# First block of a fused two-block forward pass: split projections, modulation weights on 32-column tiles, attentions begun after three slots

## The chip, the cores and the metric

The kernel runs on one core of one Trainium2 chip. The metric is device time in microseconds (us). The core has a matrix engine (TensorE, PE in the views; its weight loads are listed as PEld), VectorE (DVE), ScalarE (ACT), GpSimd (POOL) and SyncE (SP), which issues the loads. All five run their own instruction streams and meet at semaphores.

## The reference, cut to what matters

Two blocks of two layers each follow one another on an activation of 256 tokens by 1024 features. The change touches the first block alone:

```python
def first_block(x, c, ada_w, ada_b, norm_g, ab_w_in, ab_w_out, ..., c_w_in, c_w_out, c_sink, final_g):
    cs = jax.nn.silu(c)
    for layer in range(DEPTH):                                  # 2 layers
        mod = cs @ ada_w[layer] + ada_b[layer]                  # 1024 -> 3072, one row
        shift, scale, gate = jnp.split(mod, 3, axis=-1)
        h = rms_norm(x, norm_g[layer]) * (1.0 + scale[:, None, :]) + shift[:, None, :]
        if layer % 2 == 0:  y = even_mixer(h, ab_w_in, ab_w_out, ...)
        else:               y = odd_mixer(h, c_w_in, c_w_out, c_sink)
        x = x + gate[:, None, :] * y
    return rms_norm(x, final_g)
```

`even_mixer` projects h to 4096 features, runs 8 heads of a banded attention with three patterns (A) and 4 heads of a differential attention (B, two score maps each), multiplies by `silu(g)` and projects back. `odd_mixer` projects to 2560 features, runs 16 banded heads with a sink, gates and projects back. Everything is float32.

## The kernel before, in words

**Slots.** Every weight is cut into slots of 1 MB (128 partitions by 2048 values), in the order of `NAMES`, and SyncE loads them one after another into a ring of four (`RING`); slot n+4 is issued when TensorE has signalled slot n (`slot_done`). Of the first block: `ada0_*` and `ada1_*` (12 each, the modulation vector of a layer), `even0..15` and `even_out0..3`, `odd0..9` and `odd_out0..3`. Those of the second block begin with L0. Besides these, SyncE issues x (1 MB) ahead of slot 5, and constants of 0.88 MB ahead of slot 7 and 0.56 MB ahead of slot 8.

**A slot on TensorE.** In the first block a projection slot is 16 float32 matmuls of 128x128 by 256 (`pe_features`, or `pe_tokens` where tokens go to partitions). The trace has each float32 matmul as two records. An `ada` slot is 8 such matmuls with a broadcast vector as the stationary side; VectorE takes the diagonal of each 128x128 half (`dve_mod_slot`).

**Split slots.** The second block writes each float32 as a rounded high part plus a low part and multiplies high by high, high by low and low by high, 48 matmuls of one record each (`pe_split`). For it ScalarE casts the slot to `w_split` (two buffers, `act_highs`; the cast for split slot w waits until split slot w-2 is done), and VectorE subtracts and leaves the low part in the ring (`dve_lows`). `act_slot` and `dve_slot` take a slot's result and then cast and subtract ahead; `dve_slot` subtracts first (up to the next slot), and takes the result then. h itself comes as `h_split` (high) and `hT_rounded` (low).

**Attention as a pipeline.** `pe_attention` walks over pairs of score maps. Step k has on TensorE the scores of pair k (`sc`), the values of pair k-2 (`yv`), the transposes of pair k-1 (`tp`), and then filler slots from the table `FILL`. VectorE has in step k the bias and row minimum of pair k (`att_area`, L461), the results of the filler of step k-1, the scaling of pair k's probabilities (L476 to L486) and the product of the finished chunk (L1920). ScalarE has the filler's results, the exponentials (L428) and the copies of the transposes (L442). GpSimd builds the bias tables (L508 to L511), two heads ahead. There are 8 pairs in each of the two attentions, so steps 0 to 9.

**Order around the change.** ada0_0 to ada0_8; norm; even0 to even12; the even attention with even13 to 15 and nine ada slots as filler; sums for the norm of the differential heads; ada1_6 and 7; `even_out`; norm; odd0 to odd5; the odd attention with odd6 to 9 and ada1_9 to 11; `odd_out`; then the second block with L0sbq.

## Time and profile before

| what | us |
|---|---|
| device time, median of 3 runs (1488.1 to 1491.31) | 1490.55 |
| the profiled execution | 1490.07 |
| its span in the trace | 1488.2 |
| first even projection begins | 44.8 |
| even attention begins, after 13 slots | 134.8 |
| even_out begins, after ada1_6 and ada1_7 | 220.8 |
| odd projections begin | 256.9 |
| odd attention, from its first scores | 299.5 |
| odd_out begins | 373.0 |
| second block begins (L0sbq) | 417.9 |

The page gives busy times and shares of the span. The chain of waits in order of time gives the piece of work that held the end at each moment: a piece on TensorE means that TensorE itself was the limit there, one on another engine that TensorE waited for it. What comes after 417.9 us is the second block, which keeps its code and its slots.

### The profile page before, as it was taken

To read this page: it belongs to the slowest core of one execution; us is meant where nothing else is said; L and a number is where in the kernel's file an instruction comes from. 1 tells how busy PE (TensorE), PEld (TensorE's weight loads), DVE (VectorE), ACT (ScalarE), POOL (GpSimd) and SP (SyncE) were. 2 spreads that over 40 slices of the span, in tenths; PEclk is the share of its full clock that TensorE was granted. 3 is DMA by queue.
4 is the path that set the end of the run, shared out by engine and by line. 5 is a ranking of instruction groups with operands and counts; after the bars stand their busy time and mean duration, and the time that the engine had idled before them with its cause. 6 is when DMAs were issued, how large, how long until landed. Compare 5 with 4: busy or idle time off the path is not lost.

```text
span 1488.2 us, 21174 instructions
## 1 busy us (share of the span) xinstructions
PE 1419.3 (95%) x8756; PEld 1243.8 (84%) x8756; DVE 795.6 (53%) x1156; ACT 623.2 (42%) x821; POOL 195.2 (13%) x130
## 2 busy tenths in 40 slices
PE   8999999998989999999999999899998999999997
PEld 7888788875879898898888888798998888888885
DVE  1102663067164777944775554436778637755543
ACT  1202322044237566621464443476567223644432
POOL 1002310043000034123020000000240231200000
PEclk9999999998989999999999999999999999999999
DMA  9544354433223443301445555333333203454551
GB/s 363 203 166 142 142 207 157 145 114 114 99 103 139 142 147 137 142 29 57 147 179 184 177 191 190 121 142 142 142 142 114 85 29 116 170 195 171 192 178 55
DMA packets 30048, 216.23 MB, mean 145 GB/s; under 512 B 3328, under 2 KB 3584, under 8 KB 4096
## 3 DMA queue, kind: packets, MB, share of 16 engines
q1 hardware_dynamic: 29952, 214.87, 40.1%
q8 instruction: 69, 1.13, 0.3%
q14 instruction: 27, 0.22, 0.0%
HBM read 213.81 MB, written 1.05 MB: 144 GB/s over the span
## 4 chain that ended last, share of the span: by engine, by line
PE 88%; DVE 5%; ACT 4%; issue 2%; DMA 0%; POOL 0%; DVEq 0%; SPq 0%; ACTq 0%
PE pj L520 59%; PE yv L520 13%; PE sc L520 9%; PE tp L520 4%; PE tp L411 1%; ACT w_split L627 1%; DVE rw L1281 1%; PE tp L1458 1%; DVE ring_rounded L636 1%; DVE att_area L461 1%; ACT att_area L428 0%; DVE rstd L683 0%; DMA ring<-weights 0%; DVE hT L685 0%; ACT probsT L442 0%
## 5 line engine op out<-in xcount | busy, mean ns | idle before, releaser
L1617 DVE TENSOR_TENSOR ring_rounded<-ring,big_rounded 128x2048 fp32r<-128x2048 f32 x62 | 142.1, 2292 | 96.0 <-ACT big_rounded L1548 95.8
L636 DVE TENSOR_TENSOR ring_rounded<-ring,w_split 128x2048 fp32r<-128x2048 f32 x68 | 163.1, 2404 | 41.6 <-ACT w_split L627 40.0
L520 PE MATMUL pj<-h_split,w_split 128*128 128x256 f32 x992 | 143.9, 298 | 15.2 <-ACT h_split L1553 10.1
L520 PEld LDWEIGHTS pj<-h_split,w_split 128*128 128x128 f32 x992 | 128.8, 197 | 25.9 <-issue 19.7
L520 PE MATMUL pj<-hT,ring 128*128 128x256 f32 x672 | 147.3, 380 | 1.7 <-DVE mod_raw L1375 1.2
L1548 ACT CAST big_rounded<-ring 128x2048 fp32r<-128x2048 f32 x66 | 125.8, 1906 | 51.3 <-PE pj L520 49.8
L520 PEld LDWEIGHTS pj<-hT,ring 128*128 128x128 f32 x672 | 126.9, 190 | 19.9 <-issue 3.0
L627 ACT CAST w_split<-ring 128x2048 fp32r<-128x2048 f32 x68 | 129.2, 1903 | 21.0 <-PE pj L520 12.9
L520 PE MATMUL pj<-h_split,ring_rounded 128*128 128x256 f32 x992 | 127.8, 282 | 0.0
L520 PE MATMUL pj<-yT,ring 128*128 128x256 f32 x512 | 118.7, 386 | 4.7 <-DVE yT L1329 2.5
L520 PEld LDWEIGHTS pj<-h_split,ring_rounded 128*128 128x128 f32 x992 | 122.6, 191 | 0.0
L520 PEld LDWEIGHTS pj<-yT,ring 128*128 128x128 f32 x512 | 96.8, 193 | 19.8 <-DVE yT L1329 2.9
L520 PE MATMUL pj<-hT_rounded,w_split 128*128 128x256 f32 x864 | 112.5, 283 | 0.0
L520 PEld LDWEIGHTS pj<-hT_rounded,w_split 128*128 128x128 f32 x864 | 107.8, 192 | 0.0
L1023 POOL TENSOR_TENSOR big<-big 128x512 f32<-128x512 f32 x16 | 31.1, 1946 | 494.1 <-DVE big L962 480.8
L520 PE MATMUL pj<-ring,cs 128*128 128x256 f32 x384 | 88.2, 388 | 7.7 <-DMA ring<-weights 6.4
L520 PEld LDWEIGHTS pj<-ring,cs 128*128 128x128 f32 x384 | 74.2, 195 | 18.5 <-issue 8.3
L1350 DVE COPY big<-pj 128x512 f32<-128x512 f32 x11 | 7.6, 689 | 117.5 <-PE pj L520 117.4
L520 PE MATMUL pj<-big_rounded 128*128 128x512 f32 x176 | 69.1, 393 | 0.0
L520 PE MATMUL sc<-big_rounded 128*128 128x512 f32 x176 | 69.0, 392 | 0.0
L1346 ACT ACTIVATE big<-pj 128x512 f32<-128x512 f32 x23 | 13.7, 597 | 123.6 <-PE pj L520 123.6
L510 POOL TENSOR_SCALAR first_block<-first_block 128x384 f32<-128x384 f32 x24 | 28.0, 1168 | 268.0 <-DVE stat L467 124.1
(312 smaller groups left out, 2374.8 us busy)
## 6 DMA issues: line engine op xcount, KB each, us to landing
ring<-weights SPq DMA_DIRECT2D x200, 1024.0 KB, 4.8
xT<-x_t SPq DMA_DIRECT2D x1, 1024.0 KB, 7.0
out_t<-hT SPq DMA_DIRECT2D x1, 1024.0 KB, 3.9
con<-constants SPq DMA_DIRECT2D x1, 896.0 KB, 9.5
aux<-small SPq DMA_DIRECT2D x1, 832.0 KB, 6.4
first_block<-constants SPq DMA_DIRECT2D x1, 576.0 KB, 9.9
level_masks_sb<-levels SPq DMA_DIRECT2D x1, 448.0 KB, 6.0
con<-constants SPq DMA_DIRECT2D x1, 128.0 KB, 5.1
```

The source lines that it names most:

```text
L411: last = nc.tensor.transpose(tp[m["t"] % 2][:, jt * SEQ + it * P:jt * SEQ + (it + 1) * P], probs[:, m["g"] % 4, it, jt * P:(jt + 1) * P], ...
L461: ins = nc.vector.tensor_tensor_reduce(probs[:, m["g"] % 4, it], sc[m["g"] % 2][:, it * SEQ:(it + 1) * SEQ], table[:, P - it * P:P - it * ...
L510: pool.do(nc.gpsimd.tensor_scalar(bias0[:, :], C("dist"), m["slope"], None, ALU.mult))
L520: return nc.tensor.matmul(out, lhsT, rhs, start=start, stop=stop, skip_group_check=True)
L627: act.post(nc.scalar.copy(w_split[:, w % 2], ring[:, idx % RING]), s["w_high"])
L636: dve.post(nc.vector.tensor_tensor(ring_r[:, at], ring[:, at], w_split[:, w % 2].bitcast(F32), ALU.subtract), s["w_low"])
L1023: pool.tell(nc.gpsimd.tensor_tensor(d, b, b[:, :, n - 1:n].to_broadcast([P, 512 // (2 * n), 2 * n]), ALU.subtract), s["hgrn_diff"])
L1281: dve.tell(nc.vector.tensor_tensor(rw[:, kind, T * NH:(T + 1) * NH], quarters((sc + tp)[(2 * kind + T) % 4]), C("before" if kind < 2 else ...
L1346: free(act, nc.scalar.activation(dst, b[:, :], ACT.Copy, scale=scale), name)
L1458: last = nc.tensor.transpose(tp[j % 2][:, (2 * c + T) * P:(2 * c + T + 1) * P], by_token(j, T)[:, c * P:(c + 1) * P], C("ident"))
L1548: act.tell(nc.scalar.copy(w_high(i), ring[:, w_at(t, i) % RING]), s["ffn_high"])
L1617: e.tell(engine.tensor_tensor(w_low(t, i), w, value(w_high(i)), ALU.subtract), signal)
```

## The change

It has five parts.

1. All projection slots of the first block (16 even, 4 even_out, 10 odd, 4 odd_out) become split slots, with casts on ScalarE and subtractions on VectorE. h is shifted by ScalarE straight into `h_split`, and VectorE makes its low part. The attention's output chunks are split into `y_high` (in `big2`) and `y_low` (in `yT_rounded`) as they are finished.
2. The ada slots come as pairs that share one bank of 512 columns' sums: each half has 4 of the 8 row blocks, and each of its 16 matmuls has 32 output columns and 128 moving columns, on column tile j of 4. VectorE takes four diagonals of 32 per pair.
3. The even attention begins after even0, 2, 4 (and even1 as filler of step -1), the odd one after odd4, 5, 0. The others are filler in the steps, with waits (`NEEDED`) on what a pair needs. ada0_8 goes from ahead of the projections into step 3.
4. The subtractions for the next filler group are made ahead in the first block too (`AHEAD`).
5. The final product of the differential heads is made per chunk.

```diff
 FILL = {
-    "even": {-1: ["even12"], 0: ["even13"], 1: ["ada0_9"], 2: ["even14"], 3: ["ada0_10"], 4: ["ada0_11", "ada1_0"],
-             5: ["even15"], 6: ["ada1_1", "ada1_2"], 7: ["ada1_3"], 8: ["ada1_4"], 9: ["ada1_5"],
-             EVEN_TAIL: ["ada1_6"], EVEN_TAIL + 1: ["ada1_7"]},
-    "odd_norm": {0: ["ada1_8"]},
-    "odd": {0: ["odd6"], 1: ["odd7"], 2: ["odd8"], 3: ["odd9"], 4: ["ada1_9"], 5: ["ada1_10"], 6: ["ada1_11"]},
+    "even": {-1: ["even1"], 0: ["even3", "even12"], 1: ["even6", "even8"], 2: ["even5", "even13"],
+             3: ["even10", "ada0_8", "ada0_9"], 4: ["even7", "even9"], 5: ["ada0_10", "ada0_11", "even14"],
+             6: ["even11"], 7: ["ada1_0", "ada1_1"], 8: ["ada1_2", "ada1_3"], 9: ["ada1_4", "ada1_5"],
+             EVEN_TAIL: ["even15"], EVEN_TAIL + 1: ["ada1_6", "ada1_7"]},
+    "odd_norm": {0: ["ada1_8", "ada1_9"]},
+    "odd": {0: ["odd1"], 1: ["odd6"], 2: ["odd2"], 3: ["odd7"], 4: ["odd3"], 5: ["odd8"], 6: ["odd9"],
+            8: ["ada1_10"], 9: ["ada1_11"]},
...
-CHAIN = ("stick", "moba", "hgrn", "rwkv")
-GROUPS = [(phase, k, FILL[phase][k]) for phase in CHAIN for k in sorted(FILL[phase])]
-AHEAD = {phase: {} for phase in CHAIN}
-for (phase_, k_, _), (_, _, next_) in zip(GROUPS, GROUPS[1:]):
-    if "branch" not in next_[0]:
+GROUPS = [(phase, k, at[k]) for phase, at in FILL.items() for k in sorted(at)]
+AHEAD = {phase: {} for phase in FILL}
+for (phase_, k_, _), (next_phase, _, next_) in zip(GROUPS, GROUPS[1:]):
+    if "branch" not in next_[0] and (phase_ == next_phase or phase_ in ("stick", "moba", "hgrn")):
         AHEAD[phase_][k_] = next_[-1]
+EVEN_FIRST, ODD_FIRST = ("even0", "even2", "even4"), ("odd4", "odd5", "odd0")
+NEEDED = {"even": {0: ("even0", "even2"), 2: ("even1", "even3", "even4"), 4: ("even5", "even6", "even8"),
+                   6: ("even7", "even9", "even10"), 8: ("even11",)},
+          "odd": {0: ("odd4", "odd0"), 2: ("odd1", "odd5"), 4: ("odd2",), 6: ("odd3",)}}
...
-    add("ada0_", 9)
-    add("even", 12)
+    add("ada0_", 8)
+    names.extend(EVEN_FIRST)
     names.extend(FILL_ORDER["even"])
     add("even_out", 4)
     names.extend(FILL_ORDER["odd_norm"])
-    add("odd", 6)
+    names.extend(ODD_FIRST)
...
-    return name[0] == "L" and not any(part in name for part in ("branch", "ffn", "down"))
+    return not any(part in name for part in ("ada", "branch", "ffn", "down"))
...
+    if "ada" in n:
+        return ada_part(n) % 2
...
+    put("quad", i[:, None] % 32 == np.arange(32)[None, :])
...
+                for name in NEEDED.get(phase, {}).get(k, ()):
+                    evacuated(pe, name)
...
+        def act_y_high(act, chunk):
+            act.post(nc.scalar.copy(y_high[:, chunk], yT[:, chunk]), s["y_high"])
+
+        def dve_y_low(dve, chunk):
+            dve.take(s["y_high"])
+            dve.post(nc.vector.tensor_tensor(yT_r[:, chunk], yT[:, chunk], value(y_high[:, chunk]), ALU.subtract),
+                     s["y_low"])
...
+                if phase in NEEDED and 3 <= k < 3 + len(placed(phase)):
+                    m = placed(phase)[k - 3]
+                    act.eng.wait_ge(y_out, m["u"] + 1)
+                    act_y_high(act, m["chunk"])
...
+                if phase in NEEDED and 4 <= k < 4 + len(placed(phase)):
+                    dve_y_low(dve, placed(phase)[k - 4]["chunk"])
...
+        def act_h_shift(act):
 
             for k in range(KC):
-                act.take(s["h_scaled"])
-                act.post(nc.scalar.activation(hT[:, k], hT[:, k], ACT.Identity, bias=mod[:, k:k + 1]), s["h_ready"])
+                act.take(s["h_to_split"])
+                act.post(nc.scalar.activation(hh[:, k], hT[:, k], ACT.Identity, bias=mod[:, k:k + 1]), s["h_high"])
+
+        def dve_norm_shift(dve, name):
+
+            dve.take(s["norm_root"])
+            dve.do(nc.vector.reciprocal(rstd[:, 1], rstd[:, 0]))
+            for k in range(KC):
+                dve.post(nc.vector.scalar_tensor_tensor(hT[:, k], xT[:, k], mod[:, 8 + k:9 + k], rstd[:, 1], ALU.mult,
+                                                        ALU.mult), s["h_to_split"])
+            dve_lows(dve, IDX[name])
+            for k in range(KC):
+                dve.take(s["h_high"])
+                dve.post(nc.vector.scalar_tensor_tensor(hT_r[:, k], hT[:, k], mod[:, k:k + 1], value(hh[:, k]), ALU.add,
+                                                        ALU.subtract), s["h_low"])
...
-            for m in range(2):
-                ins = nc.vector.tensor_tensor_reduce(diag[:, :], b[:, m * P:(m + 1) * P], C("ident"), 1.0, 0.0, ALU.mult,
-                                                     ALU.add, mod_raw[:, 2 * i + m:2 * i + m + 1])
-                if m == 0:
+            i = ada_part(name)
+            for m in range(4):
+                ins = nc.vector.tensor_tensor_reduce(diag[:, 0:32], b[:, m * 32:(m + 1) * 32], C("quad"), 1.0, 0.0,
+                                                     ALU.mult, ALU.add, mod_raw[:, 2 * i - 2 + m:2 * i - 1 + m])
+                if m < 3:
...
-                idx = IDX[name]
-                pe_open(pe, name)
-                for k in range(KC):
-                    last = matmul(bank_of(name)[:, 0:SEQ], cs[:, k:k + 1].to_broadcast([P, P]), slot(idx)[:, k],
-                                  k == 0, k == KC - 1)
+                idx, half = IDX[name], ada_part(name) % 2
+                w = ring[:, idx % RING].rearrange("p (k j n) -> p k j n", k=4, j=4)
+                if half == 0:
+                    pe_open(pe, name)
+                else:
+                    arrived(pe.eng, idx)
+                for k in range(4):
+                    for j in range(4):
+                        at = 4 * half + k
+                        last = matmul(bank_of(name)[32 * j:32 * j + 32, 0:P], cs[:, at:at + 1].to_broadcast([P, 32]),
+                                      w[:, k, j], at == 0, at == KC - 1)
...
+            pe.take(s["y_high"], 4)
+            pe.take(s["y_low"], 4)
+            for i in range(2):
+                pe_split(pe, f"even_out{i}", (y_high, yT_r), ks=range(KC // 2))
+            for i in range(KC // 2):
+                if i < 2:
+                    pe_split(pe, f"even_out{i}", (y_high, yT_r), (s["y_high"], s["y_low"], 1) if i == 0 else None,
+                             ks=range(KC // 2, KC))
+                else:
+                    pe_split(pe, f"even_out{i}", (y_high, yT_r))
...
+            fill(act, act_slot, "even", EVEN_TAIL)
+            act_highs(act, IDX["even_out1"])
+            for chunk in range(4, KC):
+                act.take(s["mixed"])
+                act_y_high(act, chunk)
+            for i in range(KC // 2):
+                evacuated(act, f"even_out{i}")
+                act_square(act, i, scr)
+                act_highs(act, min(IDX[f"even_out{i}"] + 2, IDX["even_out3"]))
...
+                dve.post(nc.vector.tensor_tensor(yT[:, 4 + h], yT[:, 4 + h], ge[:, 4 + h], ALU.mult), s["mixed"])
+            dve_lows(dve, IDX["even_out0"])
+            for chunk in range(4, KC):
+                dve_y_low(dve, chunk)
+            dve_lows(dve, IDX["even_out1"])
+            for i in range(KC // 2):
+                dve_residual(dve, "even_out", lambda ch: mod[:, 16 + ch:17 + ch], (i,))
+                dve_lows(dve, min(IDX[f"even_out{i}"] + 2, IDX["even_out3"]))
             dve_mod(dve, 1)
-            dve_norm(dve, hT, mod, 8, s["h_scaled"])
+            dve_norm_shift(dve, ODD_FIRST[0])
```

Two places show where instructions go. VectorE at the start, around the last of the modulation slots that the norm needs; `diag` is the product with the mask, `mod` the scale and shift, L683 (L709) the norm's reciprocal. Before:

```order
L1375 ISA diag,mod_raw<-pj,con 128x128 [waits slot_done,bank_free0]
L1375 ISA mod_raw 128x1
L1375 ISA diag,mod_raw<-pj,con 128x128 [waits dve_step]
L1375 ISA mod_raw 128x1
L1389 TENSOR_TENSOR mod<-mod_raw,vec 128x16 [waits bank_free1]
L1391 SCALAR_TENSOR_TENSOR mod<-mod,vec 128x8 [waits dve_step]
L683 RECIPROCAL rstd<-rstd 128x256 [waits norm_root,x_landed,dve_step]
```

After:

```order
38 L655 TENSOR_TENSOR ring_rounded<-ring,w_split 128x2048 [waits w_high,bank_free0]
39 L1383 ISA diag,mod_raw<-pj,con 128x32 [waits slot_done]
40 L1383 ISA mod_raw 128x1
41 L1383 ISA diag,mod_raw<-pj,con 128x32 [waits dve_step]
42 L1383 ISA mod_raw 128x1
43 L1383 ISA diag,mod_raw<-pj,con 128x32 [waits dve_step]
44 L1383 ISA mod_raw 128x1
45 L1383 ISA diag,mod_raw<-pj,con 128x32 [waits dve_step]
46 L1383 ISA mod_raw 128x1
47 L1397 TENSOR_TENSOR mod<-mod_raw,vec 128x16 [waits bank_free1]
48 L1399 SCALAR_TENSOR_TENSOR mod<-mod,vec 128x8 [waits dve_step]
49 L709 RECIPROCAL rstd<-rstd 128x256 [waits norm_root,x_landed,dve_step]
```

The subtraction for even0, which waits for its cast and so for its load, now stands ahead of the last diagonals.

VectorE between the even attention and even_out, where the differential heads are normalized (two reciprocals of `scr`) and gated. Before, with the diagonals of ada1_6 between the reciprocals (not shown) and those of ada1_7 behind them:

```order
211 L1908 RECIPROCAL scr<-scr 128x512 [waits diff_root,dve_step]
...
216 L1908 RECIPROCAL scr<-scr 128x512 [waits bank_free0]
...
221 L1911 SCALAR_TENSOR_TENSOR yT<-big,cols,scr 128x256 [waits bank_free1]
222 L1911 SCALAR_TENSOR_TENSOR yT<-big,cols,scr 128x256 [waits dve_step] x3
223 L1913 TENSOR_TENSOR yT<-yT,big 128x1024 [waits dve_step]
224 L718 SCALAR_TENSOR_TENSOR xT<-pj,mod,xT 128x256 [waits slot_done,mixed]
```

After:

```order
230 L1938 RECIPROCAL scr<-scr 128x512 [waits diff_root,dve_step]
231 L1367 SCALAR_TENSOR_TENSOR big<-big,pj 128x512 [waits gate_tanh,dve_step]
232 L1938 RECIPROCAL scr<-scr 128x512 [waits bank_free0]
233 L655 TENSOR_TENSOR ring_rounded<-ring,w_split 128x2048 [waits w_high,dve_step]
...
248 L1941 SCALAR_TENSOR_TENSOR yT<-big,cols,scr 128x256
249 L1943 TENSOR_TENSOR yT<-yT,big 128x256 [waits dve_step]
250 L442 TENSOR_TENSOR yT_rounded<-yT,big_rounded 128x256 [waits y_high] x4
251 L655 TENSOR_TENSOR ring_rounded<-ring,w_split 128x2048 [waits w_high]
252 L726 SCALAR_TENSOR_TENSOR xT<-pj,mod,xT 128x256 [waits slot_done]
```

Between the first reciprocal and the first residual (L718, now L726) there now stand the gate of even15, the subtractions for even_out0 and even_out1 and four low parts of y; four diagonals of ada1_6/7 and the chunks 4 to 7 one by one are among the rows left out.

## Rows read from the trace of the kernel before

**Rows 1.** The page, part 1: busy us, share of the span, instructions.

```profile
PE 1419.3 (95%) x8756; PEld 1243.8 (84%) x8756; DVE 795.6 (53%) x1156; ACT 623.2 (42%) x821; POOL 195.2 (13%) x130
```

**Rows 2.** The chain of waits, 0 to 520 us: start, us, what (xrecords).

```profile
40.70 0.29 DVE diag L1375
...
41.77 1.76 DVE rstd L683
...
44.79 90.02 PE pj L520 x416
...
145.07 3.46 PE pj L520 x16
...
213.88 20.72 PE pj L520 x96
...
250.25 0.50 DVE xT L718
...
256.89 41.68 PE pj L520 x192
...
299.46 1.13 PE sc L520 x8
...
372.99 16.23 PE pj L520 x64
...
406.53 0.49 DVE xT L718
...
417.91 27.06 PE pj L520 x192
...
454.47 5.72 PE pj L520 x48
```

**Rows 3.** Groups by form, PE: xcount, busy us, mean ns, idle before, releasers.

```profile
L520 PE MATMUL pj<-hT,ring 128*128 128x256 f32 x672 | 147.3, 380 | 1.7 <-DVE mod_raw L1375 1.2 <-ACT hT L709 0.5
...
L520 PE MATMUL pj<-ring,cs 128*128 128x256 f32 x384 | 88.2, 388 | 7.7 <-DMA ring<-weights 6.4 <-DVE mod_raw L1375 1.3
```

**Rows 4.** The slot's cast, by tile, 376 to 640 us: ns min/median/max.

```profile
L627 ACT CAST w_split<-ring x28: 1898/1903/1915, 392.2 to 615.0; 128x2048 fp32r<-128x2048 f32 x28
```

**Rows 5.** The slot's subtraction, by tile, 376 to 640 us.

```profile
L636 DVE TENSOR_TENSOR ring_rounded<-ring,w_split x28: 2282/2292/3265, 399.0 to 619.2; 128x2048 fp32r<-128x2048 f32 x28
```

**Rows 6.** DMA of the first 60 us, GB/s in 40 slices of 1.5 us.

```profile
GB/s 0 176 371 390 418 421 426 426 311 169 421 410 426 426 311 235 367 425 419 417 405 443 435 437 404 350 120 66 289 399 448 404 104 0 11 164 415 120 0 44
```

**Rows 7.** The page, part 6: the weight loads, count, KB each, us to landing.

```profile
ring<-weights SPq DMA_DIRECT2D x200, 1024.0 KB, 4.8
```

**Rows 8.** Stretches: us, busy of PE, PEld, DVE, ACT, POOL, granted clock (PEclk), DMA, GB/s.

```profile
418.00:422.00 4.00, 4.00 (x14) 3.25 (x14) 4.00 (x13) 2.37 (x7) 0.00 (x0) 0.50 0.00 0
366.00:374.00 8.00, 6.66 (x26) 3.74 (x25) 1.40 (x5) 1.17 (x2) 0.00 (x0) 0.50 0.01 2
```

**Rows 9.** Timeline of PE: start, us; sixteen records on two row tiles, and what follows.

```profile
563.09 1.16 PE L520 MATMUL yv<-big 64*128 64x128 f32 x16
564.18 1.10 PE L520 MATMUL pj<-h_split,w_split 128*128 128x256 f32 x7
```

**Rows 10.** Timeline of DVE behind the even attention.

```profile
215.43 3.35 DVE L1908 RECIPROCAL scr<-scr 128x512 f32<-128x512 f32 x1 [2.08 <-ACT scr L1817]
...
225.62 1.22 DVE L1913 TENSOR_TENSOR yT<-yT,big 128x1024 f32<-128x1024 f32 x1
```

**Rows 11.** Timeline of DVE and POOL in step 4 of the odd attention.

```profile
337.91 0.42 DVE L461 CUSTOM_DVE_ANT_0 att_area<-sc,first_block 128x256 f32<-128x256 f32 x1 [2.64 <-PE sc L520]
...
340.46 0.69 DVE L1359 SCALAR_TENSOR_TENSOR big<-big,pj 128x512 f32<-128x512 f32 x1
...
342.83 1.00 POOL L511 TENSOR_TENSOR first_block<-first_block 128x384 f32<-128x384 f32 x1
...
342.92 0.92 DVE L476 TENSOR_TENSOR stat<-stat 128x2 f32<-128x2 f32 x1
...
345.31 0.42 DVE L461 CUSTOM_DVE_ANT_0 att_area<-sc,first_block 128x256 f32<-128x256 f32 x1
```

154 lines of the change are left out of this document (64 added, 90 removed).

## The prediction

> **What bounds the kernel now.** I read the page's busy shares first: TensorE is busy for 95% of the span, with VectorE at 53% and ScalarE at 42% [rows 1]. So a change pays where it shortens TensorE's own stream, and costs where it makes TensorE wait for the two engines that still have room on average, though perhaps not in a given step. Next comes the chain of waits in order of time [rows 2]: pieces of TensorE follow one another from 44.79 us on, and they date the stages. 13 projection slots take 90.02 us, or 6.92 each; an ada slot takes 3.46; a split slot of the second block (48 records) takes 5.72. Then the groups by form [rows 3]: TensorE sat idle ahead of the projections for 1.7 us and ahead of the ada slots for 7.7, of which 6.4 is the first load. Engines that are not on the chain matter for what they would do next to added work, and I take those from single steps below. The second block, from 417.91 us on, keeps its slots, and I leave it at its time.
>
> **Prices.** Split slot: 6.92 - 5.72 = 1.20 us less on TensorE. It adds a cast of 1.90 us on ScalarE [rows 4] and a subtraction of 2.29 us on VectorE, at most 3.27 [rows 5]. The first one behind a norm pays more, as its h comes chunk by chunk and the clock is down: the first four split slots of the second block took 27.06 us, which is 4.2 over 4 x 5.72 [rows 2].
>
> Pair of ada slots: now 2 x 3.46 = 6.92 us; then 64 records of 128 moving columns on four column tiles. No row has four tiles. Ends: full overlap, a quarter, 1.73 us; none, 6.92. The nearest row is sixteen records of 128 columns on two row tiles in 564.18 - 563.09 = 1.09 us [rows 9], 68 ns each. A full-width record of 256 columns costs 6.92/32 = 216 ns, so 128 columns are 108 and two overlapped tiles 54; the row lies 14 ns above. Estimate for four tiles: 27 + 14 = 41 ns, times 64 = 2.6 us. I take 2.6, with 4.4 (64 x 68) as the dear side.
>
> What speaks against this price is a floor per instruction. The Trainium skill (TensorE: Matmul & The Clock Gate, section "Wait — 56ns, not 53.3ns?") has ≈62 ns per MATMUL where the sequencer's microcode decodes. By it a pair would be 4.0 us and the sum below some 8 us worse; the row of 68 ns allows it and doesn't prove it, since two tiles can't go below 54.
>
> **Stage by stage.** Each is before, then after.
>
> *Start to first projection, 44.8 -> 40.0.* TensorE no longer paces the ada slots; loads do. 426 GB/s is the rate that the loads reach when SyncE isn't held [rows 6], so I take 420. VectorE's order has the subtraction for even0 ahead of the diagonals of ada0_7, hence ahead of the norm. even0 is the ninth slot: 9 x 1.05 MB [rows 7], x 1.05, constants and vectors 1.8, is 12.3 MB, or 29.2 us behind a start of 2 = 31.2. Cast 1.9, subtraction 2.3, diagonals 1.3, scale 0.4, reciprocal 1.76, first chunk and its shift 1.0: 39.9. Without that order it would be about 34. -4.8.
>
> *Projections ahead of the even attention, 90.0 -> 4 x 5.72 + 4.2 = 27.1.* -62.9; nine slots go to the next stage. Cast and subtraction (4.2) fit beside a slot, and the low part is wanted in a slot's last third only.
>
> *Even attention with its filler and sums, 213.88 - 134.81 = 79.1 -> 107.0.* Less 3 x 6.92 and 9 x 3.46 leaves 27.2 for attention, sums and old waits. Plus 11 x 5.72 = 62.9 and 5 pairs, 13.0: 103.1. In a two-slot step VectorE has some 9 us (four bias operations of 0.42 with their gaps 1.9, two subtractions 4.6, scaling and product 2.5), with GpSimd's collisions 12, under TensorE's 14.5: hidden. New waits: steps 3 and 4 open a bank that VectorE frees only behind the bias, 0.6 each; the low part late by 0.3 in three steps; ScalarE's cast of even15, which waits for a load, ahead of the square that the sums need, 2.0. About 3.9. +27.9.
>
> *Sums to the end of even_out, 250.25 - 213.88 = 36.4 -> 44.1.* From the end of the sums, TensorE does even15 (5.7), the pair (2.6), two thirds of a half even_out0 (1.9): 10.2. VectorE: 1.6 for the root, reciprocal 3.35 [rows 10] = 4.9; the gate of even15 waits for that slot and its tanh, 7.1; reciprocal 10.5; subtraction 12.8, and TensorE has waited 2.6. Diagonals 14.1, four chunks (2.05 + 1.7; the one product for all four took 1.22 [rows 10]) 17.7, four low parts 19.5, subtraction for even_out1 21.8. TensorE, there at 15.7, waits 6.1 more. Then 0.95 + 2 x 2.85, two slots of 5.72 and two sums of 0.86: 41.6. The granted clock stands at half, the 1.2 GHz level, in two stretches behind waits of TensorE [rows 8], and the two slots that begin at 372.99 took 16.23, 2.4 over 2 x 6.92; I add that 2.4. +7.7.
>
> *Norm:* the same chain of residual, root, reciprocal and shift, 6.6; ada1_8/9 lie under it. 0.
>
> *Odd projections, 42.6 -> 21.6.* 3 x 5.72 + 0.9 for the last result as before, + 3.5: VectorE does eight chunks (3.3), the subtraction (2.3), eight low parts (3.5), and TensorE's last product ends with them, at 9.1 instead of 5.7. -21.0.
>
> *Odd attention, 372.99 - 299.46 = 73.5 -> 82.5.* This is where I see the gain go. One step of VectorE took 345.31 - 337.91 = 7.40 us, with a gate of 0.69 [rows 11]. Each step 1 to 6 now has a subtraction, 2.29, and from step 4 a low part, 0.45. Steps 0 to 6: 6.2, 8.5, 9.7, 9.0, 10.2, 9.5, 10.2 = 63.3, against TensorE's 6.8, 7.8, 5 x 8.8 = 58.6. Step 7 begun (1.1 + 63.3), the rest took 12.9 (345.31 + 2 x 7.40 = 360.1, to 372.99), and ada1_10 and 11, formerly in steps that TensorE had to spare, now stand in the last two, at half clock: +3.9. That makes 81.2. GpSimd's bias building blocks VectorE's operations with two SBUF inputs: a 128x2 sum took 0.92 us and ended with GpSimd's instruction beside it [rows 11]; the long subtraction meets it too (2.28 to 3.27 [rows 5]). 1.3 for that. +9.0; ends -2 (all hidden) and +16.
>
> *odd_out, 33.5 -> 28.6*: 4 x 1.20. -4.9.
>
> Sum: -4.8 - 62.9 + 27.9 + 7.7 - 21.0 + 9.0 - 4.9 = -49.0. As a cross-check, what TensorE drops on its path is 34 x 1.20 = 41 in projections and 11 x 3.46 - 6 x 2.6 = 22 in ada slots, the start gives 5, and 19 come back as waits. From the profiled execution's 1490.07, which is 0.5 below the median of the runs: 1441.1, so **1441**.
>
> **Rivals.**
> 1. *The waits don't come.* If subtractions hide in every step and VectorE catches up behind the sums, 19 of waits shrink to 2: 1424. For: VectorE has 47% free. Against: the order of VectorE around even15 is fixed. 15%.
> 2. *The narrow matmuls pay per record*, 68 ns or a little less: 4.4 a pair, (4.4 - 2.6) x 6 = +11 on the path: 1452. The floor per MATMUL of the page named above belongs here. 15%.
> 3. *The four column tiles don't overlap at all:* the second part does nothing, 6.92 a pair: +26, 1467. Against it: tiles by two overlap [rows 9]. 7%.
> 4. *VectorE sets every attention step*, GpSimd blocking each subtraction for its whole 0.97 and more: +1.5 in 14 steps and a colder clock: 1462. 8%.
> 5. *Slower than before:* the handshake of the two `w_split` buffers. A cast waits for the slot two before, the subtraction for the cast, and TensorE's last third for the subtraction. If ScalarE's in-order stream (exponentials, waits for transposes) puts the cast behind TensorE's need, each slot is exposed by up to 1.90 + 2.29 = 4.2. From 2.0 us a slot (68/34) nothing is left; at 4.2 the time is 1490 - 68 + 143 = 1565. Against: in the second block 28 such slots ran with no such wait on the chain, e.g. the four from 417.91 us. 2%.
>
> **How the numbers follow.** Forecast as described, 53%; rivals 15, 15, 7, 8 and 2%. The range leaves out the third and fifth and a little below the first: 1423 to 1463. Differences under 0.2% are about what a measurement of this kernel can't tell from no change. Only rival 5 ends above 1493: slower 2%, same 1%, faster 97%.
>
> **What would show it.** A pair of ada slots lasts 2.6 us in even step 3; the first projection starts at 40 with the subtraction for even0 right ahead of the last diagonals; TensorE waits some 9 us for `ring_rounded` around even_out0 and 1, with the clock at half behind it; odd steps last 9 to 10 us with VectorE busy almost throughout; the second block takes as long as before. Wrong would be: a pair over 4 us, or odd steps of 8.8 (then the conversions hide), or of more than 11.

## The result, and the profile after

The kernel after takes **1451.12 us** in the median of four runs (1449.86 to 1451.44), the kernel before, timed beside it, 1490.22 (1488.1 to 1491.31). The ratio is 0.9739, 95% interval 0.9727 to 0.9751: 39 us faster. The forecast was 1441 with a range of 1423 to 1463. The sign and the mechanism are right and the time lies in the range, 10 us above the forecast. The profiled execution took 1451.02 us, its span 1449.1.

Part 1 of the page of after, as [rows 1]:

```profile
PE 1342.8 (93%) x9684; PEld 1195.8 (83%) x9684; DVE 880.8 (61%) x1225; ACT 694.1 (48%) x872; POOL 219.1 (15%) x130
```

TensorE lost 76.5 us of busy time and the kernel 39. The rest came back as waits of TensorE: VectorE has 85 us more work and ScalarE 71. The chain of waits of after (start, us, what), answering to [rows 2], dates the stages:

```profile
33.91 1.91 ACT w_split L646
35.91 2.29 DVE ring_rounded L655
39.46 1.76 DVE rstd L709
42.42 24.50 PE pj L562 x192
...
170.87 4.82 DMA ring<-weights
175.75 1.90 ACT w_split L646
...
182.29 5.72 PE pj L562 x48
...
227.08 0.50 DVE xT L726
...
254.45 1.14 PE sc L562 x8
...
355.25 5.73 PE pj L562 x48
...
361.07 1.90 ACT w_split L646
...
373.22 26.90 PE pj L562 x192
```

A split slot of the first block takes 5.73 us where a wide one took 6.92. Four slots stand ahead of the even attention and take 24.50; before, thirteen stood there and took 90.02. Below, each stage of the prediction in us; "before" is as the prediction has it, and odd_out begins with its first product (334.01).

| stage | before | forecast | after | off by |
|---|---|---|---|---|
| start to first projection | 44.8 | 40.0 | 42.4 | +2.4 |
| projections ahead of even attention | 90.0 | 27.1 | 24.5 | -2.6 |
| even attention, filler, sums | 79.1 | 107.0 | 115.4 | +8.4 |
| sums to end of even_out | 36.4 | 44.1 | 44.8 | +0.7 |
| norm | 6.6 | 6.6 | 6.6 | 0 |
| odd projections | 42.6 | 21.6 | 20.8 | -0.8 |
| odd attention | 73.5 | 82.5 | 79.6 | -2.9 |
| odd_out | 33.5 | 28.6 | 27.0 | -1.6 |
| last residual to second block | 11.4 | 11.4 | 12.2 | +0.8 |
| second block | 1070.3 | 1070.3 | 1075.9 | +5.6 |

Two rows hold most of the miss: the even attention, and the second block, whose code the change leaves alone.

**The ada slots.** Timeline of PE in after (start, us, what, xrecords, idle ahead and what ended it), first the start, then even step 3 and odd steps 8 and 9:

```profile
6.20 1.94 PE L562 MATMUL pj<-ring,cs 128*32 128x128 f32 x32 [6.20 <-DMA ring<-weights]
...
118.05 1.95 PE L562 MATMUL pj<-ring,cs 128*32 128x128 f32 x64
119.94 1.13 PE L562 MATMUL sc<-big 64*128 64x256 f32 x8
...
329.97 1.94 PE L562 MATMUL pj<-ring,cs 128*32 128x128 f32 x32
...
333.00 1.08 PE L562 MATMUL pj<-ring,cs 128*32 128x128 f32 x32
```

64 records from 118.05 to the next piece at 119.94 are 1.89 us, or 30 ns each (59 for each matmul of the program, which leaves two records): a quarter of a full-width record of 128 columns (108) is 27. The slot at 329.97, shortly behind a wait of 5.43 us, took 1.94 instead of 1.08, with the granted clock at 0.50 for 329.9 to 331.8. The first slots of the kernel took as long, 60 ns a record, with gaps for the loads between them; there the profile gives 1.00, so that its rows don't explain it.

**From even step 5 to even_out**, timeline of PE in after:

```profile
143.11 2.65 PE L562 MATMUL pj<-h_split,w_split 128*128 128x256 f32 x16 [3.04 <-ACT w_split L646]
145.56 3.10 PE L562 MATMUL pj<-hT_rounded,w_split 128*128 128x256 f32 x16
...
154.49 2.14 PE L562 MATMUL pj<-w_split,h_split 128*128 128x256 f32 x16 [1.40 <-issue]
...
165.72 1.10 PE L562 MATMUL yv<-probsT,big 128*128 128x256 f32 x4 [0.81 <-issue]
168.06 0.88 PE L429 MATMUL tp<-con,att_area 128*128 128x128 f32 x4 [1.25 <-DVE att_area L520]
168.88 3.34 PE L562 MATMUL pj<-ring,cs 128*32 128x128 f32 x64
...
178.66 3.63 PE L562 MATMUL sc<-scr,con 128*128 128x512 f32 x4 [3.51 <-ACT scr L1832]
...
192.04 1.86 PE L562 MATMUL pj<-big_rounded,w_split 128*128 128x256 f32 x8 [2.16 <-ACT w_split L646]
...
196.53 1.23 PE L562 MATMUL pj<-big_rounded,ring_rounded 128*128 128x256 f32 x8 [0.92 <-DVE ring_rounded L655]
...
204.43 2.07 PE L562 MATMUL pj<-big_rounded,ring_rounded 128*128 128x256 f32 x8 [4.75 <-DVE ring_rounded L655]
```

The reader should see three long waits. The first is for the cast of even14. The second is for the square that the sums need, which ScalarE does behind the cast of even15; that cast itself waits for its load, which landed at 175.7. The third is for the low part of even_out1. The matmuls behind the first two take half as long again and more (3.10 against 2.08; 3.63 against 1.98 in a later kernel). The granted clock is below full there: 0.89 for 135.5 to 150.5 us, 0.54 for 178.7 to 182.3.

### The profile page after: what moved, and what is told of

The parts are those of the page before. It is cut to its first block, busy times and chain, and to the rows that moved or that the text cites. A ratio compares the mean times of both kernels' runs of the same rounds, so it can differ in the third digit from the quotient of the medians.

```text
span 1449.1 us, 23149 instructions
## 1 busy us (share of the span) xinstructions
PE 1342.8 (93%) x9684; PEld 1195.8 (83%) x9684; DVE 880.8 (61%) x1225; ACT 694.1 (48%) x872; POOL 219.1 (15%) x130
## 3 DMA queue, kind: packets, MB, share of 16 engines
q8 instruction: 77, 1.26, 0.4%
## 4 chain that ended last, share of the span: by engine, by line
PE 79%; DVE 10%; ACT 5%; issue 3%; DMA 2%; POOL 0%; DVEq 0%; ACTq 0%; SPq 0%
PE pj L562 52%; PE yv L562 13%; PE sc L562 9%; PE tp L562 4%; DMA ring<-weights 2%; DVE ring_rounded L655 2%; ACT w_split L646 1%; DVE att_area L498 1%; DVE att_area L523 1%; PE tp L429 1%; DVE rw L1289 1%; PE tp L1466 1%; DVE stat L513 1%; ACT att_area L457 0%; DVE stat L504 0%
## 5 line engine op out<-in xcount | busy, mean ns | idle before, releaser
L655 DVE TENSOR_TENSOR ring_rounded<-ring,w_split 128x2048 fp32r<-128x2048 f32 x102 | 242.8, 2385 | 83.1 <-ACT w_split L646 81.0
L562 PE MATMUL pj<-h_split,w_split 128*128 128x256 f32 x1328 | 194.5, 300 | 30.2 <-ACT h_split L704 11.2
L646 ACT CAST w_split<-ring 128x2048 fp32r<-128x2048 f32 x102 | 193.7, 1902 | 52.8 <-PE pj L562 28.0
L562 PEld LDWEIGHTS pj<-h_split,w_split 128*128 128x128 f32 x1328 | 175.0, 200 | 44.2 <-issue 37.4
L562 PE MATMUL pj<-h_split,ring_rounded 128*128 128x256 f32 x1328 | 172.7, 283 | 4.1 <-DVE ring_rounded L655 4.1
L562 PE MATMUL pj<-hT_rounded,w_split 128*128 128x256 f32 x1200 | 157.8, 285 | 0.0
L562 PE MATMUL pj<-yT,ring 128*128 128x256 f32 x256 | 60.2, 383 | 4.1 <-DVE yT L1337 2.5
L552 POOL TENSOR_SCALAR first_block<-first_block 128x384 f32<-128x384 f32 x24 | 33.9, 1411 | 188.4 <-DVE stat L504 106.4
L562 PEld LDWEIGHTS pj<-yT,ring 128*128 128x128 f32 x256 | 46.8, 190 | 11.2 <-DVE yT L1337 2.9
L562 PE MATMUL yv<-big_rounded,yT_rounded 128*128 128x512 f32 x192 | 49.8, 401 | 0.0
L562 PE MATMUL yv<-ring_rounded,yT_rounded 128*128 128x512 f32 x192 | 49.0, 397 | 0.0
```

The costliest lines, as they stand in the source:

```text
L552: pool.do(nc.gpsimd.tensor_scalar(bias0[:, :], C("dist"), m["slope"], None, ALU.mult))
L562: return nc.tensor.matmul(out, lhsT, rhs, start=start, stop=stop, skip_group_check=True)
L646: act.post(nc.scalar.copy(w_split[:, w % 2], ring[:, idx % RING]), s["w_high"])
L655: dve.post(nc.vector.tensor_tensor(ring_r[:, at], ring[:, at], w_split[:, w % 2].bitcast(F32), ALU.subtract), s["w_low"])
```

## Experiments

All ratios are to the kernel before, timed beside each kernel. Stages are read from the one execution of each kernel that was traced, and compared with after's; where that execution was not near the median of its kernel, the text says so. "Block 1" ends where the second block's first product starts (373.22 in after).

**1. Ada slots wide again (a_wide).** Both slots of a pair go side by side into one bank:

```
-for k in range(4):
-    for j in range(4):
-        at = 4 * half + k
-        last = matmul(bank_of(name)[32 * j:32 * j + 32, 0:P], cs[:, at:at + 1].to_broadcast([P, 32]),
-                      w[:, k, j], at == 0, at == KC - 1)
+for k in range(KC):
+    last = matmul(bank_of(name)[:, half * SEQ:(half + 1) * SEQ], cs[:, k:k + 1].to_broadcast([P, P]),
+                  slot(idx)[:, k], half == k == 0, half == 1 and k == KC - 1)
...
```

The diagonals go back to 128 columns (four per pair), and the weights to their layout of before.

> The kernel after with its ada slots computed wide again: the condition column broadcast to 128 columns against all 256 weight columns, both slots of a pair side by side in one bank, pairs, order and everything else as in the kernel after. The diagonals use the 128-wide identity, four per pair. Theory A (four column tiles overlap nearly fully): a pair of the kernel after took 1.89 us warm (64 records, 30 ns each), a wide one 6.92, so each of the five pairs before the sums and after them costs 5.0 more: the pair in even step 3 lasts 6.9; steps 7, 8, 9 have room on VectorE's side, so not all of it is exposed. The first eight slots pace the start again: first projection at about 45 instead of 42.4. The last two ada slots stand in odd steps where VectorE is late, 2.5 more at most. Sum +20 to +30: 1471 to 1481. Theory B (a change of only a few ns per record matters little, since the gain of this kernel is in the split projections alone): within 6 us of 1451.

1472.82 us, ratio 0.9889 (0.9876 to 0.9903): 21.7 above after, as theory A has it; theory B falls. Block 1 is 20.4 longer. By stages: start 2.7, even attention up to its sums 12.7, the norm ahead of the odd projections 2.9 (the pair under it is no longer hidden), odd attention and its projections 2.2, the rest small. Timeline of PE in a_wide, steps 5 and 9:

```profile
146.59 7.07 PE L562 MATMUL pj<-ring,cs 128*128 128x256 f32 x32
153.31 2.25 PE L562 MATMUL pj<-h_split,w_split 128*128 128x256 f32 x16
...
188.08 7.07 PE L562 MATMUL pj<-ring,cs 128*128 128x256 f32 x32
194.99 1.88 PE L562 MATMUL sc<-scr,con 128*128 128x512 f32 x4
```

A pair costs 5.0 more (6.91 from 188.08 to 194.99, against 1.89), and five of them would be 25; the even attention shows half. The other half had lain in after's waits: here TensorE waits neither for the cast of even14 nor ahead of the sums, and the two waits in step 8 are gone too (3.04 + 3.51 + 0.81 + 1.25 = 8.6 us). The matmuls behind them run at their full pace. The narrow pairs uncovered those waits.

**2. The narrow pairs alone, in the kernel before (b_narrow).** Projections wide, twelve ahead of the attention; filler `1: ada0_8/9, 2: even14, 3: ada0_10/11, 4: ada1_0/1, 5: even15, 6: ada1_2/3, 8: ada1_4/5`.

> The kernel before with part 2 of the change alone: ada slots in pairs on four column tiles of 32, projections wide as before, all twelve still ahead of the even attention. The pairs stand where the single slots stood or one step earlier (steps 1, 3, 4, 6, 8, behind the sums, under the norm, odd step 4). Theory A (a pair takes 1.9 us instead of 6.92, and part 2 is worth the same in either kernel): the wide form cost the kernel after 21.4 us (1472.8 against 1451.1, or by stages 2.7 at the start, 12.7 in the even attention, 5 in the odd one), so here about -22: 1467; start to first projection 38 to 41, projections 90 as before, even attention with its sums 64 to 70 instead of 77.3 and odd attention 69 to 72 instead of 73.5. Theory B (filler is worth something only where the chain of bias, exponentials, reciprocals and transposes doesn't wait; with little filler left, that chain sets the steps): even attention above 72, total -10 to -15: 1475 to 1479. Either theory: the second block, whose code is the same, shows 1070 to 1079 us.

1476.1 us, ratio 0.9911 (0.9895 to 0.9928), 13.7 below before. The total is theory B's, the stages are not: the even attention up to its sums took 63.1 us instead of 77.3, where theory A had 64 to 70 and theory B above 72. The traced execution saved 6.9 us up to the first projection, 14.2 in the even attention, 4.8 from its sums to even_out and 3.0 in the odd attention and behind it; it lost 2.6 in the projections, 6.9 from even_out to the odd projections (43.2 where before had 36.3) and 5.6 in the second block. Part of theory B's mechanism is there all the same: in step 8 of the even attention nothing is left that covers the chain of exponentials and transposes.

```profile
184.33 2.07 PE L523 MATMUL yv<-probsT,big 128*128 128x256 f32 x4 [3.95 <-ACT probsT L445]
```

By the total, the narrow pairs are worth 13.7 us in the kernel before and 21.7 in the kernel after. Up to the second block the two traces have nearly the same: 19.5 (417.91 to 398.46) and 20.4. Most of the difference is the second block, 5.6 longer here and 1.0 longer in a_wide than in after; its code is the same in all of them (experiments 10 and 11). So these runs don't show that the parts of the change help one another.

**3. The old order with split slots (a_old_order).** All twelve even and all six odd projections stand ahead of their attention again.

```
-EVEN_FIRST, ODD_FIRST = ("even0", "even2", "even4"), ("odd4", "odd5", "odd0")
+EVEN_FIRST, ODD_FIRST = tuple(f"even{i}" for i in range(12)), ("odd4", "odd5", "odd0", "odd1", "odd2", "odd3")
...
```

The filler (not shown) is what is left: even12 to 15, odd6 to 9 and the ada pairs, nearly in the order of b_narrow.

> The kernel after with part 3 undone: split projections and narrow ada pairs as in after, but all twelve even projections (and all six odd ones) ahead of their attention again, and only the gates and the ada pairs as filler in the steps. Theory A (the chain between TensorE's pieces of an attention step, some 7 us without filler by the odd step of 7.40 in the kernel before, sets every step that has only a pair or nothing beside it): nine slots of 5.72 = 51.5 go ahead, the even attention of 111.8 shrinks by only 35 to 42, and the odd one of 79.6 by 5 to 10 where three slots of 17.2 went ahead: +10 to +16 and +7 to +12, so 1468 to 1479. Theory B (split slots are bound by TensorE wherever they stand, and VectorE's room in the steps is what they use up): what the steps lose equals what goes ahead: within 4 us of 1451.

1457.94 us (1456.95 to 1462.54), ratio 0.9793 (0.9778 to 0.9809): the order brings 6.8 of the 39, less than theory A said and more than B. The profiled execution was the longest of the four (1462.54), so its stages show the place better than the size: projections, even attention and all that follows it up to the odd projections took 189.9 us in the old order and 191.2 in the new one; the odd projections and attention 111.4 against 100.4. So **the third part earns its gain in the odd attention only**. In the even one it saves waits for probsT (4.26, 1.08, 1.01 us in this kernel's trace) and pays for them with the waits for conversions shown above.

This kernel also prices the splitting. It differs from b_narrow in parts 1, 4 and 5 of the change, and in the steps of a few slots; it took 18.2 us less (1457.94 against 1476.1). So the 39 are some 14 for the narrow pairs, 18 for the split slots with parts 4 and 5, and 7 for the third part. Parts 4 and 5 were not run by themselves.

**4. even14 ahead of its pair (a_gate14_first).**

```
-  5: ["ada0_10", "ada0_11", "even14"],
+  5: ["even14", "ada0_10", "ada0_11"],
```

> The kernel after with even14 ahead of ada0_10 and ada0_11 in even step 5 (on all engines). In the profile of after TensorE sat idle for 3.04 us at 143.11 for the cast of even14 on ScalarE, and ran with the granted clock below full right behind it. ScalarE makes the cast for the slot two places on in the order, and the two ada slots count as places, so the cast of even14 was queued behind the exponentials of step 5. Theory A (look-ahead counted in places): even14 ahead of the pair puts the cast one place group earlier; the idle of 3.04 goes, and up to 1.7 of slow clock behind it: -2 to -4.5 us, 1446.5 to 1449. Theory B (ScalarE has no room, the wait only moves): the same idle shows at the next split slot, time within 1 us.

1448.01 us (1446.5 to 1449.48), ratio 0.9723 (0.9709 to 0.9736). The wait of 3.04 is gone, and behind it no matmul is slow:

```profile
139.02 2.15 PE L562 MATMUL pj<-h_split,w_split 128*128 128x256 f32 x16
141.00 2.08 PE L562 MATMUL pj<-hT_rounded,w_split 128*128 128x256 f32 x16
```

The even attention up to the sums took 106.3 instead of 111.8, although the wait ahead of the sums grew from 3.51 to 4.60. Sums to even_out took 1.3 more, the odd projections 1.8 more with the clock below full (0.85), and block 1 ended 3.1 earlier. Theory A holds: ScalarE casts two *places* ahead, an ada slot counts as a place, and so the cast was queued behind the exponentials of its own step.

**5. even15 in step 7 (a_gate15_early).**

```
-  7: ["ada1_0", "ada1_1"], 8: ["ada1_2", "ada1_3"], 9: ["ada1_4", "ada1_5"],
-  EVEN_TAIL: ["even15"], EVEN_TAIL + 1: ["ada1_6", "ada1_7"]},
+  7: ["even15"], 8: ["ada1_0", "ada1_1"], 9: ["ada1_2", "ada1_3"],
+  EVEN_TAIL: ["ada1_4", "ada1_5"], EVEN_TAIL + 1: ["ada1_6", "ada1_7"]},
```

> The kernel after with even15 moved from behind the sums to even step 7, and the three ada pairs that stood in steps 7 to 9 each one place later, so that ada1_4 and ada1_5 stand where even15 stood. In the profile of after the cast of even15 (a wait for its load, 1.90) stood ahead of the square that the sums need: TensorE idle 3.5 us at 173.2 to 178.7 and the sums at low clock; and behind the sums VectorE's gate of even15 stood between the root and the reciprocals. Theory A (even15 in the wrong place): the wait ahead of the sums falls to 1 or less, and the chain behind the sums loses the gate's wait of about 2 us; but less filler (1.9 instead of 5.7 and 1.9) covers root and reciprocal, so there up to 3 come back. Even attention plus sums 112 instead of 115.4 with the slot moved in: net -4 to -8 us, 1443 to 1447. Theory B (TensorE's time behind the sums is set by VectorE's own row of root, reciprocal, scale, chunks and low parts): what is gained ahead of the sums is given back behind them by idle, net within 1.5 us.

1446.99 us (1444.85 to 1449.03), ratio 0.9715 (0.9702 to 0.9728); block 1 ended 5.9 earlier. The wait ahead of the sums is gone, but what comes behind them is a third thing that neither theory named: of four narrow slots in a row TensorE does the first three in 1.08 us each, and their loads come 2.5 us apart.

```profile
176.53 1.08 PE L562 MATMUL pj<-ring,cs 128*32 128x128 f32 x32
179.02 1.08 PE L562 MATMUL pj<-ring,cs 128*32 128x128 f32 x32 [1.42 <-DMA ring<-weights]
181.50 1.08 PE L562 MATMUL pj<-ring,cs 128*32 128x128 f32 x32 [1.39 <-DMA ring<-weights]
```

**6. The orders around the sums (a_tail).** On ScalarE the square comes ahead of the cast for even15, on VectorE both reciprocals ahead of its gate; no slot moves.

```
+  if name not in ("ada1_4", "ada1_5"):
       act_highs(act, IDX[name.split(".")[0]] + 2)
...
   act.tell(nc.scalar.activation(flat(scr[:, 0:4]), flat(yb_raw), ACT.Square), s["diff_squares"])
+  act_highs(act, IDX["even15"])
...
   for i in range(2):
       dve.do(nc.vector.reciprocal(flat(scr[:, 2 * i:2 * i + 2]), flat(scr[:, 2 * i:2 * i + 2])))
+  for i in range(2):
       fill(dve, dve_slot, "even", EVEN_TAIL + i)
```

> The kernel after with two orders changed around the sums and nothing moved between steps: on ScalarE the cast for even15 comes behind the square of yb that the sums need, instead of ahead of it; on VectorE both reciprocals stand ahead of the gate of even15, instead of one on each side. In the profile of after TensorE sat idle 3.51 us ahead of the sums (load of even15 landed at 175.7, cast 1.90, square), the sums ran at the low clock (3.63), and the gate stood between the reciprocals (183.84 and 190.80, 3.35 each). Theory A (it is the order): idle ahead of the sums at most 0.7 and the sums in 2.0 us, so they end 4 us earlier; even15 starts with the end of its cast at 177.7 instead of 181.5; behind it the reciprocals end 3 to 4 us earlier and the wait of 4.75 for the low part of even_out1 shrinks to 2 or less or moves by as much; first block shorter by 3 to 7 us: 1445 to 1448. Theory B (VectorE's row of work from root to even_out1's low part has the same length whatever its order, and the next thing, the load of even_out0 and 1, is late anyway): below 1.5 us in all.

1445.1 us (1441.4 to 1447.33), ratio 0.9699 (0.968 to 0.9717), 6.0 below after: theory A, at the end of its 1445 to 1448. Block 1 is shorter by 9.4 in the trace, more than theory A's 3 to 7, but the traced execution was the fastest of the four (1441.4), 3.7 under their median.

```profile
172.47 1.98 PE L562 MATMUL sc<-scr,con 128*128 128x512 f32 x4 [0.20 <-ACT scr L1833]
176.07 2.14 PE L562 MATMUL pj<-h_split,w_split 128*128 128x256 f32 x16 [1.62 <-ACT w_split L646]
...
187.28 2.05 PE L562 MATMUL pj<-big_rounded,w_split 128*128 128x256 f32 x8 [3.39 <-DVE big L1367]
...
197.31 1.21 PE L562 MATMUL pj<-big_rounded,ring_rounded 128*128 128x256 f32 x8 [2.60 <-DVE ring_rounded L655]
```

3.51 became 0.20, with 1.62 behind the sums for the cast of even15, and the sums took 1.98 instead of 3.63. The wait for even_out1's low part fell from 4.75 to 2.60, and one of 3.39 for the gate stands where 2.16 for a cast had been: VectorE's row of work from the root on is still what TensorE waits for.

**7. The start (a_start).** VectorE does the diagonals of ada0_7 ahead of the subtraction for even0.

```
-  if "." not in name:
+  if "." not in name and name != "ada0_7":
       dve_lows(dve, IDX[name] + 1)
```

> The kernel after with one order undone on VectorE: the subtraction for even0 no longer stands ahead of the diagonals of ada0_7; they come first. In the profile of after the last ada0_7 product ended at 32.4 us, the load of even0 landed at 33.9, its cast ended at 35.8 and the subtraction at 38.2; the diagonals, the reciprocal and the first chunk followed, and the first projection began at 42.42. Theory A (order of VectorE): diagonals at about 32.5 and reciprocal, chunks by 36, first projection limited by the cast at 35.8 and by the first shifted chunk: begins at 37 to 38.5, the rest of the slot paced by chunks and the low part: even attention begins 2 to 4 us earlier, and the time falls by 2 to 4. Theory B (something else, the load or the low part of the weights, is late right behind it): first projection earlier but the end of the fourth slot moves by less than 1 us; time within 1 us of 1451.

1449.72 us (1448.32 to 1451.49), ratio 0.9735 (0.9722 to 0.9748): not told apart from after. The order was the cause of the late first projection, which now began at 37.95, inside theory A's 37 to 38.5; but the next thing was late, and the time is nearer to theory B's.

```profile
37.95 3.75 PE L562 MATMUL pj<-h_split,w_split 128*128 128x256 f32 x16 [4.22 <-ACT h_split L704]
42.30 3.78 PE L562 MATMUL pj<-h_split,ring_rounded 128*128 128x256 f32 x16 [0.59 <-DVE ring_rounded L655]
```

The subtraction now stands behind the eight chunks (39.95 to 42.2), and the first products run below the full clock: granted 0.84 for 38 to 65.4 us, where after had 0.94 for 42.4 to 66.9. Of 4.5 us, 1.5 were left at the end of the fourth slot, and 0.2 at the end of block 1, in an execution that was the longest of the four (1451.49).

**8. GpSimd's part in the odd steps (a_bias_one_op).** Each bias table that had two instructions gets one; the mask is left out of it, so this kernel computes something else and serves for its times alone.

```
-  pool.do(nc.gpsimd.tensor_scalar(bias0[:, :], C("dist"), m["slope"], None, ALU.mult))
-  ins = nc.gpsimd.tensor_tensor(out, bias0[:, :], C(m["mask"]), ALU.add)
+  ins = nc.gpsimd.tensor_scalar(out, C("dist"), m["slope"], None, ALU.mult)
```

> The kernel after with each bias table of GpSimd built by one instruction instead of two: the mask is left out of it, so the probabilities of the odd attention and of part of the even one also see later columns. It prices the collision of VectorE with GpSimd. In the odd steps of the kernel after GpSimd was busy for 4.4 us of a step of 9.6 (instructions of 1.0 to 1.2, and 3.13 beside VectorE's subtraction), and VectorE's 128x2 sums took 0.92 to 0.97 us where one alone took 0.25. Theory A (VectorE sets the odd steps, and some 0.65 us in each of two sums per step is GpSimd's): the odd attention falls from 79.6 to 73 to 76 us, the even attention by under 2. Theory B (TensorE with its 8.8 us per step sets them, or the sums wait elsewhere): odd attention 78.5 or more. Time 1444 to 1448 by A, 1450 to 1452 by B.

One run, 1445.41 us. The odd attention took 73.7 instead of 79.6, inside theory A's 73 to 76. Timelines of DVE and POOL in after, one odd step:

```profile
286.06 0.97 DVE L513 TENSOR_TENSOR stat<-stat 128x2 f32<-128x2 f32 x1
...
288.44 0.92 DVE L513 TENSOR_TENSOR stat<-stat 128x2 f32<-128x2 f32 x1
...
283.87 3.13 POOL L553 TENSOR_TENSOR first_block<-first_block 128x384 f32<-128x384 f32 x1
...
288.35 0.99 POOL L553 TENSOR_TENSOR first_block<-first_block 128x384 f32<-128x384 f32 x1
```

and of DVE with one instruction:

```profile
285.28 0.46 DVE L513 TENSOR_TENSOR stat<-stat 128x2 f32<-128x2 f32 x1
...
286.96 0.16 DVE L513 TENSOR_TENSOR stat<-stat 128x2 f32<-128x2 f32 x1
```

The sums take 0.16 to 0.46 instead of 0.92 to 0.97. A step from scores to scores was 9.86 us in after (307.70 to 317.56) and is 8.81 here (288.08 to 296.89), with no wait of TensorE inside: that is TensorE's own time. The collision works both ways: GpSimd's addition of 0.99 took 3.13 beside VectorE's subtraction of 2.29 that began at 283.85, and the first sum ended when it did (287.03 and 287.00), the second sum with the next addition (289.36 and 289.34).

**9. The last ada pair in odd step 7 (a_ada_step7).**

```
-  8: ["ada1_10"], 9: ["ada1_11"]},
+  7: ["ada1_10", "ada1_11"]},
```

> The kernel after with ada1_10 and ada1_11 together in odd step 7 instead of in steps 8 and 9. In the profile of after TensorE sat idle 5.43 us in step 8 for probsT of ScalarE, ran its next pieces at the low clock (ada1_10 1.94, transposes 1.97) and did each ada slot with nothing to hide behind. Theory A (filler belongs into the wait): the pair hides in the 5.4 us, the odd attention ends about 2.5 to 4 us earlier than the 79.6 us from its first scores to odd_out's first product. Theory B (the chain of probs and transposes sets the end anyway): below 1 us.

One run, 1452.74 us; the odd attention took 78.8 instead of 79.6, odd_out 0.7 more. Theory B. The pair does hide, but the wait of 5.43 turned into one of 3.55 ahead of the same probsT and a new one of 1.26:

```profile
328.17 1.97 PE L562 MATMUL yv<-probsT,big 128*64 128x256 f32 x8 [3.55 <-ACT probsT L471]
...
333.30 1.97 PE L562 MATMUL yv<-probsT,big 128*64 128x256 f32 x8 [1.26 <-ACT probsT L471]
```

By these waits, the chain of probs, exponentials and transposes sets the end of the odd attention, and moving filler there brings nothing.

**10 and 11. The second block (a_delay3, b_delay).** Idle work on VectorE, just ahead of the second block: two reciprocals (1.75 and 1.15 us) in the kernel after, one (about 0.5) in the kernel before.

```
+  dve.do(nc.vector.reciprocal(hT[:, 0], rstd[:, 0]))
+  dve.do(nc.vector.reciprocal(hT[:, 1, 0:160], rstd[:, 0, 0:160]))
   dve_norm_split(dve, cols, 24, rstd[:, 0])
```

> The kernel after with 2.9 us of idle work on VectorE on the chain just ahead of the second block (two reciprocals, 1.76 and about 1.15 us, of values that nobody uses, written where the next operation overwrites them). The code of the second block is unchanged, but it starts 2.9 us later. In every kernel run so far that block's instructions, the same in the same order, took 1075.8 to 1079.3 us, and in the kernel before 1070.3; the difference lies in a few stretches in which the granted clock was below full in the one and full in the other (0.94 in 463 to 494 us of after, 1.00 in the same code of before). Theory A (which stretches run at the low clock depends on when the block starts, not on what stands ahead of it): the second block takes another time than 1075.9, by over 1 us, 1070 to 1079, with its low stretches elsewhere; the total is 1451.1 + 2.9 with that difference added, 1448 to 1457. Theory B (the first block's new code leaves the chip in another state, and the second block pays for it): 1075.9 within 0.5 again, total 1454.

> The kernel before with about 0.5 us of idle work on VectorE just ahead of the second block (a reciprocal of 128x50 values that nobody uses); nothing else. In all ten variants of the kernel after or before that were profiled the second block took 1075.5 to 1079.3 us, in the kernel before alone 1070.3, though its instructions are the same; a delay of 2.9 us in the kernel after left it at 1076.2. Theory A (the moment decides: the first block of before ends by chance at a moment from which the chip grants more of the clock, and 0.5 us later it would not): the second block takes 1074 us or more, and the time rises by 4 or more, to 1494 to 1500. Theory B (what the first block runs decides, and before's leaves the chip in a better state): 1070.3 within 1, and the time is within 1.5 of before's. If A holds, 5.6 us of the kernel after's second block are no property of the change, and an undisturbed before would on average be slower than measured; if B holds, they are a cost of it.

a_delay3 took 1453.45 us (1451.83 to 1454.68), ratio 0.9754 (0.9738 to 0.977); its second block 1076.2, within 0.4 of after's: for theory B of that run. b_delay took 1491.69 us (1487.41 to 1494.07), ratio 1.0014 (1.0004 to 1.0024), where the delay itself is 0.5; the second block of the traced execution took 1073.1, between the two theories. Stretches of before, b_delay and after, each with the same code of the second block (us, busy of PE, PEld, DVE, ACT, POOL, granted clock, DMA, GB/s):

```profile
508.00:580.00 72.00, 67.62 (x596) 64.90 (x598) 58.27 (x61) 42.93 (x55) 23.83 (x14) 1.00 0.40 144
```

```profile
509.20:581.20 72.00, 67.96 (x573) 65.38 (x574) 56.81 (x61) 42.64 (x54) 22.56 (x14) 0.95 0.40 143
419.10:1492.20 1073.10, 1031.04 (x6860) 918.92 (x6860) 647.04 (x699) 514.65 (x572) 133.15 (x66) 0.99 0.39 137
```

```profile
463.30:535.30 72.00, 67.87 (x571) 65.15 (x572) 56.76 (x61) 42.76 (x54) 22.38 (x14) 0.95 0.40 143
373.20:1449.10 1075.90, 1033.79 (x6860) 920.32 (x6860) 647.13 (x699) 514.57 (x572) 133.06 (x66) 0.98 0.38 136
```

In this execution of b_delay, with the first block of before untouched and the start of the second moved by 1.2 us (0.5 of it the delay, the rest a first projection that began at 45.41 instead of 44.79), the stretch 90 to 162 us into the second block lost the clock that it lacks in after too (0.95 instead of 1.00, 573 and 571 records in 72 us instead of 596). That is 2.8 of the 5.6 us.

How much of it the shift of the moment causes stays open. One execution of each kernel was traced, and that of b_delay was the longest of eleven. Five of the eleven took 1492.87 to 1494.07 us and six 1487.41 to 1491.69, so the same kernel at the same moment has both; of the fourteen of before beside them, none took more than 1490.62. The median rose by 2.6, of which 0.5 is the delay. The other 2.8, lost later in the block, did not come in this execution of b_delay. In all twelve traced kernels with narrow ada slots or a split first block the second block took 1075.5 to 1079.3, and why is open too.

**12. Three orders together (a_combo).** The edits of 4, 6 and 7.

> The kernel after with the three edits of order that its runs spoke for, together: diagonals of ada0_7 ahead of the subtraction for even0, even14 ahead of its pair of ada slots, and the two orders around the sums (square ahead of the cast for even15, both reciprocals ahead of its gate). By stages, up to the first slot of the second block: a_tail ended the first block at 363.9 us instead of 373.2, a_gate14_first at 370.1, a_start at 373.0. Theory A (the waits are independent): 363.9 - 3.1 - 0.3, so 360.5, and with 1075.9 for the second block a span of 1436.5 and a time of 1438, at most 1443. Theory B (what one edit brings, the next wait takes, since VectorE's row of work behind the sums is full): first block 363 or more, time 1444 to 1447, as a_tail.

**1438.21 us** (1435.2 to 1438.77), ratio 0.9651 (0.9637 to 0.9666): 52 us below before and 13 below after, the fastest kernel here. Theory A holds: its time was 1438. Block 1 ended at 357.45 in the trace, 3.0 before theory A's 360.5, but the traced execution was the fastest of the four (1435.2), 3.0 under their median. Here the gain of a_start does come through: the first projection begins at 37.16 and the fourth slot ends at 62.67, 4.2 before after's, with a granted clock of 0.94 where a_start had 0.84. What still stands behind the sums is the pair of waits of a_tail, for the gate of even15 and for the low part of even_out1:

```profile
179.26 1.48 PE L562 MATMUL pj<-big_rounded,w_split 128*128 128x256 f32 x8 [3.39 <-DVE big L1367]
...
189.27 1.33 PE L562 MATMUL pj<-big_rounded,ring_rounded 128*128 128x256 f32 x8 [3.50 <-DVE ring_rounded L655]
```

## Why the prediction was right, and where it was off

**Start (+2.4).** The order that the prediction named (subtraction for even0 ahead of the diagonals) is on the chain: 35.91, then diagonals, 39.46. The mis-sized term is the load, 33.9 instead of 31.2: I had reckoned 12.3 MB at 420 GB/s from 2 us on, and by 36 us 14.06 MB had gone at a mean of 391, since the first 3.6 us move little and the loads of the next slots share the rate. TensorE waited for a load ahead of each of the first seven ada slots.

**Split slots (right).** 5.72 a slot, as forecast. The first four took 24.50 and not 27.1: the allowance of 4.2 for the first turned out 1.6 (24.50 - 4 x 5.72).

**Pair of ada slots (mis-sized, in the kernel's favour).** 1.89 instead of 2.6. I had added to full overlap (27 ns) the 14 ns that the two-tile row lies above a half; with four tiles it is 3. Rivals 2 (68 ns a record) and 3 (no overlap) are out. The floor of ≈62 ns per MATMUL that the Trainium skill (TensorE: Matmul & The Clock Gate, section "Wait — 56ns, not 53.3ns?") gives for microcode decoding is not in the records, which are 30 ns apart. Of the program's matmuls, which are 59 ns apart and so 3 under it, the traces leave it open.

**Even attention (+8.4, the largest miss).** The failed step is the term of new waits ("About 3.9"; its own parts add up to 4.1). Found were 0.32 and 0.75 twice (named, near 0.3 and 0.6), and four that I had not: 3.04 for the cast of even14, 1.40 for the start of a slot in step 6, 0.81 and 1.25 in the chain of probs in step 8, and for even15 3.51 instead of 2.0; in all 11.8. Matmuls at the low clock behind the waits cost another 4.5: 2.65 and 3.10 against 2.15 and 2.08 for even14, 3.34 against 1.95 for a pair, 3.63 against 1.98 for the sums. Cheaper pairs gave 3.5 back. I had costed the cast of even14 at nothing since "Cast and subtraction (4.2) fit beside a slot", which holds for the engine's time and not for its place in ScalarE's order. Experiments 4 and 6 showed that: two edits of order took the 3.04 and 3.3 of the 3.51 away.

**Sums to even_out (+0.7, right).** The waits of 2.16, 0.92 and 4.75 are 7.8, the forecast had 2.6 and 6.1 (its row of times is 0.1 short at 17.7). The last two are for `ring_rounded`, as forecast, with the clock at 0.50 behind the last; the first is for the cast of even_out0, which the forecast did not have on the path.

**Odd attention (-2.9, right by wrong parts).** The +9.0 had 7.7 for VectorE's own work and the last two steps, and 1.3 for GpSimd. Measured is +6.1, and experiment 8 takes 5.9 of that away by halving GpSimd's instructions. Without the collision the step is TensorE's 8.8, which is what the prediction named for conversions that hide ("odd steps of 8.8"). A long subtraction keeps GpSimd's table of the next head from ending (3.13), and so shifts GpSimd's next instruction into VectorE's short sums; this second step of the collision was missing. That the total came out near is luck: 1.3 was put down for a collision of which one edit alone took 5.9 away, and the rest, put down at 7.7, is then 0.2.

**odd_out (-1.6).** 4 x 1.20 is 4.8 and not 4.9. More weighs that the forecast kept the 2.4 us that the half clock cost before's first two slots (16.23 instead of 13.84); in after the granted clock was 1.00 from 334 to 361 us.

**Second block (+5.6, forecast 0).** The failed step is "I leave it at its time". Its instructions are those of before. The loss shows as a lower granted clock in a few stretches; half of it was seen once with before's own first block, and its cause stays open.

**Rival 5** (casts behind TensorE's need in every slot) did not come about in general, but its mechanism did, in two places: even14 and even15. Rival 1, the opposite, falls: even a_combo, with three orders changed, is 14 us above its 1424. Rival 4 (VectorE and GpSimd set every attention step) holds for the odd steps, 9.1 to 9.9 us each from step 2 on where TensorE's own time is 8.8, and not for the even ones, where TensorE's pieces mostly follow one another; its 1462 did not come. The total lies in the range partly because misses of both signs offset each other, +17.9 and -7.9 in the table.

## What to carry to other kernels

When a slot's conversion runs two places ahead on another in-order engine, count places by time and not by number: a place that has become short (here an ada slot, from 3.46 to 1 us) brings the conversion behind whatever that engine does in the step. And price a faster filler by the waits it uncovers, stage by stage; five narrow pairs saved 25 us of TensorE's time in the even attention and 12.7 of the stage, and three edits of order that leave the work as it is brought 13 more. Where two kernels are set side by side stage by stage, use executions near their medians: those of a_tail and a_combo were 3 to 4 us under.

## What the runs showed of the hardware that I had not expected

- Float32 matmuls on four column tiles of 32 overlap almost fully: 64 records in 1.89 us, 30 ns each, where a quarter of a full-width record (108) is 27.
- VectorE and GpSimd hold each other up in both directions: a 128x2 sum took 0.92 to 0.97 us instead of 0.16, and GpSimd's addition of 0.99 us took 3.13 beside a VectorE subtraction of 2.29. One instruction less of GpSimd per bias table took 5.9 off the odd attention's 79.6 us.
- The same second block, instruction for instruction, took 1070.3, 1073.1 and 1075.9 us in one execution each of before, b_delay and after, with a granted clock of 0.99, 0.99 and 0.98, and eleven executions of b_delay spread over 6.7 us: a comparison of two kernels at the 0.2 to 0.4% level holds such differences too.
